# Two weight loads moved ahead of the wait for the gathers, and twelve more filler matmuls, in a decoder layer with a mixture of experts

## The reference

```python
p_group = softmax(hf @ w_group);  g_sel = argmax(p_group)      # 4 groups
le = logits_e[g_sel];  top_v, top_i = top_k(le, 2)             # 2 of the 8 experts of the group
gate = g_w * softmax(top_v)
ys = (silu(xb @ w_gate[e]) * (xb @ w_up[e])) @ w_down[e]       # 1024 -> 512 -> 1024, for each expert's rows
out = segment_sum(ys * row_w, row_tok)                         # back to the rows' own places
```

## Time and profile before

| | us |
|---|---|
| median of the runs | 1128.93 |
| the profiled execution's own time | 1128.53 |
| its span in the trace | 1126.8 |
| TensorE busy in the span | 1086.9 |
| VectorE, ScalarE, GpSimd busy | 441.9, 330.1, 171.1 |
| mean rate of the DMAs | 260 GB/s |

### The profile page before, as it was taken

One profiled execution on the slowest core, in us unless ns is written; L12 is line 12 of the kernel. 1 busy time (PEld: TensorE's weight loads), 2 busy tenths in 40 slices (PEclk: granted clock), 3 DMA queues, 4 the chain that ended last, 5 costly groups with the idle time before them and its releaser, 6 DMA issues.

```text
span 1126.8 us, 26824 instructions
## 1 busy us (share of the span) xinstructions
PE 1086.9 (96%) x11604; PEld 792.3 (70%) x11604; DVE 441.9 (39%) x832; ACT 330.1 (29%) x648; POOL 171.1 (15%) x149
## 2 busy tenths in 40 slices
PE   5999999999999989999899999999999999999995
PEld 5999999966665549989766666666666666666663
DVE  5326654368875543355722212212222222122121
ACT  6322232256775552213311111111111111111111
POOL 0001200599200000000011111111111111111110
PEclk9999999999999999999999999999999999999998
DMA  7357784000116368465789999999999999999992
GB/s 236 106 151 210 213 272 142 1 14 2 38 64 198 113 225 276 142 238 197 275 313 403 384 383 387 392 380 384 392 374 390 386 386 389 387 388 387 390 359 36
DMA packets 85694, 293.03 MB, mean 260 GB/s; under 512 B 13375, under 2 KB 44799, under 8 KB 59957
## 3 DMA queue, kind: packets, MB, share of 16 engines
q1 hardware_dynamic: 78405, 273.69, 65.0%
q0 software_dynamic: 7168, 17.58, 6.6%
HBM read 272.98 MB, written 42.87 MB: 280 GB/s over the span
## 4 chain that ended last, share of the span: by engine, by line
PE 92%; DVE 2%; DMA 2%; ACT 2%; issue 1%; SPq 0%; POOL 0%; ACTq 0%; POOLq 0%
PE bank L2078 13%; PE bank L2486 11%; PE bank L2490 10%; PE bank L2308 9%; PE bank L2494 8%; PE bank L2520 5%; PE bank L2524 5%; PE bank L2528 4%; PE bank L2120 4%; PE bank L2285 3%; PE bank L2249 3%; PE bank L2158 3%; PE bank L2465 2%; PE bank L2506 1%; PE bank L2375 1%
## 5 line engine op out<-in xcount | busy, mean ns | idle before, releaser
L2486 PE MATMUL bank<-w_ring,xeT 128*32 128x256 f32 x1536 | 342.6, 380 | 0.0
L2490 PE MATMUL bank<-w_ring,xeT 128*32 128x512 f32 x1536 | 265.8, 594 | 0.7 <-ACT xeT L1491 0.7
L2486 PEld LDWEIGHTS bank<-w_ring,xeT 128*32 128x32 f32 x1536 | 166.5, 110 | 54.1
L2520 PE MATMUL bank<-w_ring,hT 128*32 128x256 f32 x768 | 171.7, 380 | 0.0
L2494 PE MATMUL bank<-w_ring,xeT 128*32 128x256 f32 x1536 | 155.9, 379 | 0.0
L1960 DVE SCALAR_TENSOR_TENSOR hid<-sgl,gtab,bank 96x256 f32<-96x256 f32 x32 | 21.9, 685 | 337.6 <-ACT sgl L1497 337.6
L2524 PE MATMUL bank<-w_ring,hT 128*32 128x512 f32 x768 | 133.2, 595 | 1.6 <-ACT hT L1503 1.6
L2078 PE MATMUL bank<-w_hi,xh 128*128 128x256 f32 (+1 forms) x432 | 124.7, 289 | 0.0
L2078 PE MATMUL bank<-w_lo,xh 128*128 128x256 f32 (+1 forms) x432 | 121.8, 282 | 0.0
L2078 PE MATMUL bank<-w_hi,xl 128*128 128x256 f32 (+1 forms) x432 | 121.7, 282 | 0.0
L1699 DVE TENSOR_TENSOR_SCAN keep<-keep,unseen 128x1024 f32<-128x1024 f32 (+7 forms) x64 | 92.2, 1472 | 42.3 <-ACT keep L1282 42.2
(11 more groups left out here) (275 smaller groups left out, 1628.1 us busy)
## 6 DMA issues: line engine op xcount, KB each, us to landing
w_ring<-in_w_gate SPq DMA_DIRECT2D x64, 1024.0 KB, 30.1
w_ring<-in_w_up SPq DMA_DIRECT2D x64, 1024.0 KB, 27.4
w_ring<-in_w_down SPq DMA_DIRECT2D x64, 1024.0 KB, 29.6
k_scr<-in_cache_k SPq DMA_DIRECT2D x32, 256.0 KB, 3.2
v_scr<-in_cache_v SPq DMA_DIRECT2D x32, 256.0 KB, 3.5
pgk<-k_scr SPq DMA_DIRECT2D x32, 256.0 KB, 4.1
w_raw<-in_w_in SPq DMA_DIRECT2D x7, 1024.0 KB, 6.9
pgv<-v_scr SPq DMA_DIRECT2D x4, 1024.0 KB, 6.3
```

Of the source, the lines that this page charges most:

```text
L2486: return pe.matmul(up_right_ps(i, g), xeT[i][:, k, rows_of(g)], w[1][:, k, FA:F], start=first and g != 1, stop=ends, skip_group_check=True)
L2490: pe.matmul(gate_ps(i)[rows_of(g), :], xeT[i][:, k, rows_of(g)], w[0][:, k, :], start=first, stop=ends, skip_group_check=True)
L2520: return pe.matmul(y_right_ps(g), hT[:, ft, rows_of(g)], w[:, ft, DA:D], start=first and g != 1, stop=ends, skip_group_check=True)
```

## The change

Two edits. SyncE loads parts 7 and 8 before it waits for the two gathers, where it loaded them after; the two waits now stand right ahead of part 9, and behind the waits for the stores of `y_all` and the last router product. And the last group of fillers is of 22 matmuls instead of 10.

```diff
@@ SyncE
+            for q in (7, 8):
+                load_part(q)
+
+            sp.wait_ge(s_yst, 16 * NT)
+            sp.wait_ge(s_lgp, NT)
             for i in range(2):
                 sp.wait_ge(s_gl[i], 16)
-            for q in (7, 8):
-                load_part(q)
-            sp.wait_ge(s_yst, 16 * NT)
-            sp.wait_ge(s_lgp, NT)
             load_part(9)
@@ TensorE
             keep_warm(5)
             tables(3)
             counts()
-            keep_warm(10)
+            keep_warm(22)
```

More of the change, by code:

```diff
@@ L980, in _ @@
                     load_part({3: 2, 7: 5}[t])
-            for i in range(2):
-                sp.wait_ge(s_gl[i], 16)
             for q in (7, 8):
@@ L987, in _ @@
             sp.wait_ge(s_lgp, NT)
+            for i in range(2):
+                sp.wait_ge(s_gl[i], 16)
             load_part(9)
```

## The result

The changed kernel takes 1138.28 us (median of four runs, 1134.55 to 1139.28) against 1128.91 us: 1.0078 of before, interval 1.006 to 1.0095 (a ratio with its interval is worked out over all runs and is not the quotient of the two medians). Measured again beside the experiments it was 1137.88 us, 1.0061 (1.0041 to 1.008). Forecast were 1132.1 us and a range up to 1135.5: right in the sign, wrong in the size. The profiled execution took 1134.95 us, 6.42 us more than that of before; its span is 1133.1 us. It is one of the quickest: the record lists 23 executions of this kernel, from 1134.55 to 1140.6 us with a median of 1137.66, and only one of them is quicker.

A forecast was written before the change was run, and what follows sets the result against it. TensorE's experts were taken as the bound, rigid behind their start. That start is the later of fillers' end (570.2) and gather's landing (569.7): +3.0, plus 0.2 us, on the median 1128.93 gives 1132.1 us; range 1130.3 to 1135.5.

The forecast's parts named there:

- What bounds the kernel: Experts: TensorE is the bound and waits for no weight; about 558.3 us follow the first gate product, unchanged.
- a sign of being wrong: Experts: time from first gate product to end differing by over 1 us would mean weights or clock mattered.
- Rival 3: Expert weights: they were the bound, so earlier loading makes it faster, 1121.1 us at best, 1125 likely; chance 0.07.
- The first packet, 4.2 us behind the issue: First gather beside weights: its first packet comes 4.2 us after issue, at 567.2 us, instead of 1.6 us after.
- The landing of the gather, "Value taken: landing at 569.7 us": First gather, issued at 563.03 us among moved weights: lands at 569.7 us, between ends of 566.7 and 572.8.
- rival 1: First gather: late beside weights, 8 to 9.8 us after issue, and sets the start; 1133 to 1137 us; chance 0.13.
- the rest run nearly alone: First gather after its first packet: weights run out at 568 to 569 us, leaving 2.1 us plus a short share.
- The fillers, 3.0 us: Ahead of the first transposes: 24 added rows at 0.125 us cost 3.0 us, ending at 570.2 us.
- The stores of the routing, cost 0: Last stores of `n_scr` and `y_all`, ahead of the weights in the queue: cost 0, at worst 1.3 us, covered.
- The fall of the clock behind a wait: First products after TensorE idles for the gather: half speed for a few us, up to +3 us.
- The rule on turns between queues: First gather: engines alternate between queues packet by packet, so it loses about half its rate, landing near 568.7 us.

The follow-up runs named there:

- after_again: The changed kernel itself, unaltered, profiled and run once more beside the experiments: 1137.88 us, 1.0061 of before.
- e4: Kernel before, with only part 7 (two DMAs, 2.1 MB) loaded ahead of the wait for the gathers, 10 fillers: 1129.73 us, 1.0 of before.
- e6: Changed kernel, with part 9 also loaded ahead of the wait for the gathers (6.3 MB instead of 4.2 MB): 1138.1 us, 1.0069 of before.
- e10: Changed kernel, but GpSimd issues the second gather only once the first has landed: 1136.75 us, 1.0053 of before.
- e2: Kernel before, with 22 fillers instead of 10 and SyncE's order unchanged: 1132.14 us, 1.002 of before.
- e1: Changed kernel with 10 fillers instead of 22, so SyncE's new order alone: 1137.37 us, 1.0057 of before.
- e8: Changed kernel with 10 fillers and the second half of part 8 loaded behind the waits, three DMAs ahead: 1135.07 us, 1.0041 of before.
- e5: Kernel before, with 6 fillers instead of 10 and SyncE's order unchanged: 1131.43 us, 1.0015 of before.
- e9: Kernel before, with 16 fillers instead of 8 in the first group and 12 instead of 10 in the last: 1129.5 us, 1.0 of before.

## Why the prediction was wrong

- **What bounds the kernel: right.** No wait of TensorE for weights appears in the changed kernel either, and in its first profile the stretch behind the first product is the same to 0.1 us. In after_again it is 2.4 us longer, which the prediction had named as a sign of being wrong; the clock did that, not the weights. e4 shows that earlier weights gain nothing. Rival 3 is out.
- **The first packet, 4.2 us behind the issue: right.** It came 4.4 us behind it, at 568.29 for an issue at 563.87.
- **The landing of the gather, "Value taken: landing at 569.7 us": this step failed.** It was 573.33 us, 9.46 us behind the issue, which is rival 1 (given 0.13); the median lies 1.3 us above even that rival's 1137. The working let "the rest run nearly alone" in 2.1 us once the weights ran out; the rest took 5.2 us. The term was 2.5 us from first packet to landing, and measures 5.0 to 5.2. The third gather of before was the nearest row for a gather beside weights, and was set aside for having a longer backlog behind it. Its landing, too, was read too early, at 9.8 us at most, from a window that ended at 578.5 us: the last of its sixteen increments comes at 578.95, 10.25 us behind the issue. e6 shows that the backlog's length beyond 4 MB doesn't matter (9.20 us with 6.3 MB loaded ahead), e10 that the second gather is about 1 us of it at most.
- **The fillers, 3.0 us: right by e2** (2.3 us by the ratio, 2.6 on the chain). In the changed kernel they ended at 571.7 instead of 570.2 us, because they began 0.85 us later and the clock was still at 0.58 from 568 to 570 us: 8.04 us for 44 rows where the sum had 7.3. In the trace they are hidden behind the gather: the wait is 4.9 us with 10 fillers (e1) and 1.7 or 3.0 with 22. The times are too coarse to show it: 7.1 us by e1 alone and 1.9 by e2 alone make 9.0, and both edits together cost 8.2 to 9.4.
- **The stores of the routing, cost 0: right.** They took 5.7 and 5.8 us instead of 4.6 and 4.7, and were through at 560.9 us, 2.9 us ahead of the gather's issue. That came 0.84 us later than in before, behind the table: 0.26 us of it lie already ahead of the weights (the last store of `n_scr` at 554.77 instead of 554.51 us), and the rest came with the low clock, as 5 fillers took 2.41 us instead of 1.72 and the table products began at 561.71 instead of 560.86. Nothing shows that the change caused this.
- **The fall of the clock behind a wait** stood in rival 1 at up to 3 us, and costs 1.1 to 2.5 us in six profiles. The sum had no such term. For the profiled execution, where the clock didn't fall, the gather alone makes the miss: the forecast for it was 1131.7 us, and the first product came 3.2 us later than forecast (574.95 instead of 571.75), which gives the 1134.95 measured to 0.1 us. From 1132.1 to the median of 1138 it takes these 3.2 us and up to 2.5 us of clock. How often the clock falls in unprofiled runs, and so how these two split the median, stays open.
- **The rule on turns between queues** from the Trainium skill ("DMA: Bandwidth & Descriptors", "Queues, rings and completion order") would have had the landing near 568.7 us. The measurement, 573.33 us, differs by 4.6 us, of which 0.84 are the later issue, and decides: packets of both queues pass in the same stretch once they flow, but neither the late first packet nor the late last one follows from taking turns.

## What to carry to other kernels

An idle memory just ahead of a small gather is free room only for what is through when the gather is issued: here 2.1 MB cost nothing (e4), 3.1 MB 0.4% (e8). Count how much is left at that moment, and take the gather's time from one that ran beside a full queue, whole, not from one alone. When all loads wait for the compute engine already, loading sooner buys nothing, and fillers that bridge the new wait can at most keep the clock, while they cost their length wherever the wait is not there.

## What the runs showed of the hardware

- A gather of up to 96 rows took 3.60 to 3.85 us without weights beside it in three profiles (before, e5, e9) and 4.97 in one (e2), where one of the sixteen increments came 1.2 us behind the others.
- With 0.39 MB of weights queued at its issue it took 3.75 us (e4), with 1.55 MB 7.23 (e8), with 2.2 to 2.8 MB 8.46 to 9.66 (six profiles), and with 4.67 MB 9.20 (e6).
- Its first packet came 1.9 us behind the issue without such a backlog, and 4.36 to 4.43 us behind it in all seven profiles with 2.2 MB or more.
- The granted clock fell to 0.50 (1.2 GHz) in or shortly behind waits of 1.4 to 4.9 us that were followed by eight transposes and a wait of 0.7 us, in six of eight profiles, and stayed there for up to 6 us while products ran; behind waits of 1.1 and 1.7 us in the other two it did not fall.
- The same kernel scatters by 6 us from run to run. In the profiles 4 us of scatter lie ahead of the change, with a fall of the clock between 400 and 460 us in all eight that are late there.
